# Thin products laid record by record among dense ones, in two stacked blocks of a fused three-layer model

## The reference

```python
# first block, twice: an RG-LRU branch and a sparse attention branch
h = rms_norm(x, norm_g); z = h @ w_in
y_a = rg_lru(causal_depthwise_conv(rg_x, conv_w, conv_b), ...) * silu(rg_gate)
y_b = nsa(q, k_c, v_c, k_s, v_s, k_w, v_w, br_gate, ...) * silu(nsa_gate)
x = x + concatenate([y_a, y_b]) @ w_out
# inside nsa: keys and values of 32 tokens at a time, every 16 tokens,
# go through w1 (2048 x 128) and w2 to 15 compressed keys and values for each of 2 groups
# second mixer: 8 heads of RWKV-7, 8 heads of attention with forget gates
q, k, v, f = split_cols(p_fox, FOX_SPLITS)          # f has 8 columns: the forget logits
bonus = jnp.sum(r_h * k_h * r_k, axis=-1, keepdims=True) * v_h
y = (y + bonus.reshape(B_, T_, RW_DIM)) * g
# then hierarchical_moe: 64 experts of 1024 x 512, top 2
```

## Time and profile before

| | |
|---|---|
| median of three runs | 1480.6 us (1480.16 to 1481.89) |
| the profiled execution's own time | 1476.84 us |
| its span, first to last instruction | 1475.1 us |
| PE busy | 1110.9 us, 75% |
| weight loads busy | 803.1 us, 54% |
| DVE, ACT, POOL busy | 344.5, 215.9, 68.4 us |
| mean granted TensorE clock | 0.901 |
| transferred | 463.41 MB at 314 GB/s |
| chain that ended last | DMA 54% of the span, PE 8% |

### The profile page before, as it was taken

The page is one execution under the profiler, slowest core; times in us unless marked ns, Lnnn a source line. Parts: engine busy times, 40 slices in busy tenths (PEclk is TensorE's granted clock), DMA queues, the critical chain, the costliest instruction groups (busy, mean ns, idle before and its releaser), DMA issues.

```text
span 1475.1 us, 35657 instructions
## 1 busy us (share of the span) xinstructions
PE 1110.9 (75%) x15914; PEld 803.1 (54%) x15914; DVE 344.5 (23%) x997; ACT 215.9 (15%) x594; POOL 68.4 (5%) x119
## 2 busy tenths in 40 slices
PE   7999999999998989866665666556665666556555
PEld 4886588654886757744444444444444444444443
DVE  2553236420574353111110111011101110111111
ACT  1162106310152111100000000000000000000000
POOL 1100010000110110000000000000000000000000
PEclk9999999999999889998888888888888888888898
DMA  8742234215110099999999999999999999999997
GB/s 285 267 137 91 88 114 172 87 65 180 58 58 4 4 393 394 427 428 428 428 428 429 428 428 429 430 427 428 430 429 427 427 431 428 428 427 431 427 427 320
DMA packets 69029, 463.41 MB, mean 314 GB/s; under 512 B 14789, under 2 KB 18278, under 8 KB 44390
## 3 DMA queue, kind: packets, MB, share of 16 engines
q1 hardware_dynamic: 64784, 459.76, 75.7%
q10 hardware_dynamic: 4182, 2.72, 0.7%
HBM read 461.41 MB, written 1.05 MB: 314 GB/s over the span
## 4 chain that ended last, share of the span: by engine, by line
DMA 54%; PE 8%; issue 0%; DVE 0%; ACT 0%; SPq 0%; POOLq 0%; DVEq 0%; POOL 0%
DMA weight_slots<-in_exp_w_down_dram 54%; PE bank L2347 4%; PE bank L2338 1%; PE bank L2330 1%; PE bank L2312 0%; PE bank L2298 0%; PE bank L2364 0%; ACT work_region L2268 0%; SPq L2182 0%; DVE normed_features L2469 0%; PE bank L2318 0%; DVE tokens L2547 0%; POOLq L2222 0%; DVE tokens L2529 0%; DVE tokens L2532 0%
## 5 line engine op out<-in xcount | busy, mean ns | idle before, releaser
L2338 PE MATMUL bank<-weight_slots,work_region 128*32 128x128 f32 x5120 | 184.2, 304 | 125.1 <-DMA weight_slots<-in_exp_w_up_dram 100.7
L2338 PEld LDWEIGHTS bank<-weight_slots,work_region 128*32 128x32 f32 x5120 | 158.3, 122 | 152.4 <-DMA weight_slots<-in_exp_w_up_dram 111.0
L2347 PE MATMUL bank<-weight_slots,work_region 128*32 128x256 f32 x1376 | 111.2, 477 | 90.4 <-DMA weight_slots<-in_exp_w_down_dram 89.0
L2338 PE MATMUL bank<-work_region 128*32 128x128 f32 x2560 | 92.7, 306 | 61.7 <-DMA work_region<-in_exp_w_up_dram 52.3
L2347 PEld LDWEIGHTS bank<-weight_slots,work_region 128*32 128x32 f32 x1376 | 57.2, 131 | 129.9 <-issue 90.5
L2338 PEld LDWEIGHTS bank<-work_region 128*32 128x32 f32 x2560 | 79.7, 123 | 75.4 <-DMA work_region<-in_exp_w_up_dram 57.4
L2268 ACT COPY work_region<-bank 128x256 f32<-128x256 f32 x64 | 23.8, 372 | 603.3 <-PE bank L2347 603.3
L2504 DVE TENSOR_SCALAR work_region<-work_region 128x128 f32<-128x128 f32 x128 | 38.5, 343 | 281.4 <-PE bank L2355 281.4
L534 PE MATMUL bank<-weight_slots,normed_features 128*128 128x512 f32 (+2 forms) x288 | 101.4, 509 | 2.3 <-DVE normed_features L792 2.3
L2347 PE MATMUL bank<-work_region 128*32 128x256 f32 x672 | 58.1, 499 | 45.2 <-DMA work_region<-in_exp_w_down_dram 44.5
L2515 DVE TENSOR_TENSOR work_region<-work_region,bank 128x128 f32<-128x128 f32 x64 | 23.9, 373 | 284.7 <-PE bank L2338 284.7
(11 more groups left out here) (429 smaller groups left out, 1218.4 us busy)
## 6 DMA issues: line engine op xcount, KB each, us to landing
weight_slots<-in_exp_w_up_dram SPq DMA_DIRECT2D x43, 2048.0 KB, 41.0
weight_slots<-in_exp_w_down_dram SPq DMA_DIRECT2D x43, 2048.0 KB, 40.7
weight_slots<-in_exp_w_gate_dram SPq DMA_DIRECT2D x43, 2048.0 KB, 41.7
work_region<-in_exp_w_gate_dram SPq DMA_DIRECT2D x21, 2048.0 KB, 41.8
work_region<-in_exp_w_up_dram SPq DMA_DIRECT2D x21, 2048.0 KB, 41.0
work_region<-in_exp_w_down_dram SPq DMA_DIRECT2D x21, 2048.0 KB, 40.6
weight_slots<-in_w_in_dram SPq DMA_DIRECT2D x16, 2048.0 KB, 10.0
weight_slots<-in_w_out_dram SPq DMA_DIRECT2D x6, 2048.0 KB, 8.4
```

The lines of the kernel that those rows point to most:

```text
L2338: mm = nc.tensor.matmul(B[bank][BLK * j:BLK * (j + 1), 0:P], x[:, c], w[u][:, c, j * P:(j + 1) * P], start=c == 0, stop=c == KC - 1, tile_ ...
L2347: mm = nc.tensor.matmul(B[7][BLK * j:BLK * (j + 1), 0:256], hidt[u][:, BLK * k:BLK * (k + 1)], w_down[u][:, k, j * 256:(j + 1) * 256], sta ...
```

## The change

Matmuls of few columns are issued between the matmuls of a dense product. The products are the same; their order on PE, and three waits, change.

- The last two of the four RG-LRU projections are written out chunk by chunk, and each chunk is followed by two matmuls of a compression: `compress(0)` goes with i = 2, `compress(1)` with i = 3. The waits for z, for ACT's copies out of B[0] and B[1], and for w1 move ahead of them. Nothing stands any more between the transposes and `score(0)`, nor between `lru_gates(0)` and `lru_gates(1)`.
- `rg_gate` is cut into single `features` products: the first goes behind `score(0)`, the second stays behind `turn_p(0)`, the third and fourth are mixed with the compressed scores of group 0 and 1, one chunk and one thin matmul in turn. `weigh(2)` and `weigh(3)` go behind them.
- In the second mixer each chunk of the value projection is followed by a matmul of the forget logits, and the wait for the low-rank weights moves ahead of it.
- The last quarter of the attention's output product (FO3) is done as chunk 2, half of the bonus, chunk 3, the other half.

```diff
                 for i in range(CT):
-                    mm = features(B[2 + i // 2][:, i % 2 * T:(i % 2 + 1) * T], chunk(RGX_S, 512), slice(i * P, (i + 1) * P))
-                    if i % 2:
-                        mm.then_inc(S["rgx_done"], 1)
+                    v = i - 2
+                    if v == 0:
+                        pe.wait_ge(S["z_ready"], was("z_ready") + 1)
+                        pe.wait_ge(S["qk_copied"], was("qk_copied") + 12)
+                    if v >= 0:
+                        pe.wait_ge(mem["w1_loaded"][v], weights)
+                    for c in range(KC):
+                        mm = nc.tensor.matmul(B[2 + i // 2][:, i % 2 * T:(i % 2 + 1) * T], chunk(RGX_S, 512)[:, c, i * P:(i + 1) * P], ht[:, c, :],
+                                              start=c == 0, stop=c == KC - 1)
+                        if c == KC - 1 and i % 2:
+                            mm.then_inc(S["rgx_done"], 1)
+                        if v >= 0:
+                            some = compress(v, range(2 * c, 2 * c + 2))
+                    if v == 1:
+                        some.then_inc(S["comp1_done"], 1)
...
-                pe.wait_ge(S["z_ready"], was("z_ready") + 1)
-                compress(0)
                 pe.wait_ge(S["qkt_ready"], was("qkt_ready") + 2)
                 score(0)
+                pe.wait_ge(S["qkt_ready"], was("qkt_ready") + 4)
+                pe.wait_ge(loaded[RGG_S], weights)
+                rg_gate(0)
                 pe.wait_ge(mem["small_in"], weights * 9)
                 pe.wait_ge(S["cv_ready"], was("cv_ready") + CT)
                 lru_gates(0)
-                compress(1).then_inc(S["comp1_done"], 1)
...
                 turn_p(0)
-                pe.wait_ge(loaded[RGG_S], weights)
-                rg_gate(0)
+                rg_gate(1)
                 turn_p(1)
...
-                rg_gate(1)
-                weigh(2)
-                weigh(3)
                 pe.wait_ge(S["kct_ready"], was("kct_ready") + 1)
                 for g in range(NG):
                     r = slice(64 * g, 64 * g + 64)
                     if g:
                         pe.wait_ge(S["cmp_scores"], was("cmp_scores") + 1)
-                    for m in range(MT):
-                        for j in range(HPG):
-                            at = g * P + (m * HPG + j) * 16
-                            mm = nc.tensor.matmul(B[1][:, at:at + NB], qt[r, m, j], kct[r, 0:NB], start=True, stop=True)
+                    for c in range(KC):
+                        i, (m, j) = 2 + g, divmod(c, HPG)
+                        gate = nc.tensor.matmul(B[0][:, i % 2 * T:(i % 2 + 1) * T], chunk(RGG_S, 512)[:, c, i * P:(i + 1) * P], ht[:, c, :],
+                                                start=c == 0, stop=c == KC - 1)
+                        at = g * P + (m * HPG + j) * 16
+                        mm = nc.tensor.matmul(B[1][:, at:at + NB], qt[r, m, j], kct[r, 0:NB], start=True, stop=True)
+                    if g:
+                        gate.then_inc(S["rgg_done"], 1)
                     mm.then_inc(S["cmp_scores"], 1)
+                weigh(2)
+                weigh(3)
...
             for m in range(MT):
-                mm = tokens(m, B[2][:, m * NH:(m + 1) * NH], w, slice(2 * LORA + P, LORA_W))
+                for c in range(KC):
+                    of = ht[:, c, m * P:(m + 1) * P]
+                    mm = nc.tensor.matmul(B[m][:, :], of, chunk(FV_S)[:, c], start=c == 0, stop=c == KC - 1)
+                    if c == KC - 1:
+                        mm.then_inc(S["fv_done"], 1)
+                    mm = nc.tensor.matmul(B[2][:, m * NH:(m + 1) * NH], of, w[:, c, 2 * LORA + P:], start=c == 0, stop=c == KC - 1)
...
+            fox_half(3, (2,))
+            bonus_of(0, B[item % 8])
+            end(fox_half(3, (3,)))
+            end(bonus_of(1, B[item % 8]))
```

More of the change, by code:

```diff
@@ L579, in _, with compress @@
                 pe.wait_ge(loaded[RGX_S], first_of_two)
-                for i in range(CT):
-                    mm = features(B[2 + i // 2][:, i % 2 * T:(i % 2 + 1) * T], chunk(RGX_S, 512), slice(i * P, (i + 1) * P))
-                    if i % 2:
-                        mm.then_inc(S["rgx_done"], 1)
+                def compress(v, some):
+                    for i in some:
+                        at = 448 + v * NG * NB
+                        mm = nc.tensor.matmul(B[1][:, at:at + NG * NB], w1_c[:, v, i], z[:, v, i], start=i == 0, stop=i == LP - 1)
+                    return mm
+                for i in range(CT):
+                    v = i - 2
[13 more added lines that the diff above has]
+                        some.then_inc(S["comp1_done"], 1)
                 pe.wait_ge(S["qk_ready"], was("qk_ready") + 1)
@@ L591, in _ @@
                     t.then_inc(S["qk_transposed"], 1)
[L593 to L598, removed]
                 def lru_gates(g):
@@ L604, in lru_gates, with rg_gate @@
                             mm.then_inc(S["lru_gates_done"], 1)
[L606 to L609, removed]
+                def rg_gate(i):
+                    mm = features(B[0][:, i % 2 * T:(i % 2 + 1) * T], chunk(RGG_S, 512), slice(i * P, (i + 1) * P))
+                    if i % 2:
+                        mm.then_inc(S["rgg_done"], 1)
                 def nsa_gate(m):
@@ L672, in _ @@
                 lru_gates(0)
-                compress(1).then_inc(S["comp1_done"], 1)
                 pe.wait_ge(S["tr_ready"], was("tr_ready") + CT)
                 lru_gates(1)
-                pe.wait_ge(S["qkt_ready"], was("qkt_ready") + 4)
                 score(1)
@@ L1398, in _ @@
                 pe.wait_ge(loaded[s], 16 * (DEPTH * uses + 1))
-                for m in range(0 if s == FV_S else 1, MT):
-                    if bank + m == 7:
-                        pe.wait_ge(S["params_ready"], 1)
-                    tokens(m, B[bank + m][:, :], chunk(s), slice(0, 512)).then_inc(done, 1)
+                if s == FV_S:
+                    continue
+                if bank == 6:
+                    pe.wait_ge(S["params_ready"], 1)
+                tokens(1, B[bank + 1][:, :], chunk(s), slice(0, 512)).then_inc(done, 1)
             pe.wait_ge(loaded[LORA_S], 16 * (DEPTH * 2 + 3))
@@ L1663, in _, with bonus_of @@
                 of_blocks(f"F5{m}", G[:, m], Q[:, m])
-            fox_last(3)
-            pe.wait_ge(S["rk_ready"], CT)
-            out = bank("BONUS")
-            for m in range(MT):
+            def bonus_of(m, out):
                 for i in range(CT):
@@ L1670, in _ @@
                     mm = nc.tensor.matmul(out[:, at:at + 2], rk[:, i, m * P:(m + 1) * P], const("head_pick"), start=True, stop=True)
-            end(mm)
+                return mm
+            pe.wait_ge(S["rk_ready"], CT)
+            item = ORDER.index("BONUS")
+            pe.wait_ge(*taken(item - 8))
+            fox_half(3, (2,))
+            bonus_of(0, B[item % 8])
+            end(fox_half(3, (3,)))
+            end(bonus_of(1, B[item % 8]))
             for m in range(MT):
```

## The result

The changed kernel takes 1490.1 us (median of 8 runs, 1485.4 to 1497.9), the kernel before on the same chip 1480.8 (8 runs). The ratio is 1.0063, with a 95% interval of 1.0041 to 1.0085: 9.3 us slower. I had forecast 1472.7 and a range up to 1480. The profiled execution is of 1490.2 us, span 1488.4; that of before was one of its faster ones (span 1475.1), so between the two profiles there are 13.3 us and not 9.3.

What follows compares the result with a forecast made beforehand. PE's path ahead of SP's weight release was taken as the bound, with DMA fixed behind it. Gains 3.25 + 1.5 + 4.7 + 0.1 = 9.55 us, less one clock fall of 1.7, gave -7.9: 1472.7 us, range 1467 to 1480.

Steps and rivals of the forecast that it cites:

- (e): Second half of each layer, turn_p(2) to turn_p(7) with scores mixed into the gate: gains 3.25 us (layer 0), 1.5 (layer 1).
- (a): Interleaving on PE: each dense-to-thin change saves 0.083 us, about 80 changes, 6.6 us less PE work.
- rival 1: Several weight loads run ahead under dense records, so more thin loads vanish: about 1467 us; chance 0.06.
- (b): PE clock: mixtures are over half dense, so none of eight half-clock stretches is expected, 13.7 us.
- rival 2: Clock falls return at the new waits or stay in the mixtures: 1477 to 1482 us, no change; chance 0.14.
- (c): Layer 1, first half: ACT's chain sets the pace, 15.0 us from lru_gates(0) to turn_p(2); 0.3 us gained.
- (d): Layer 0, first half: same offsets as layer 1, turn_p(2) at 92.45 against 94.46, 2.0 us gained.
- Rival 4: Gain doesn't arrive: ACT's chains 3 us longer in each layer, or later waits eat as much; 1479 us; chance 0.08.
- (f): Second mixer: logits end 1.25 us earlier and the 96 records behind them run at full clock; gain 4.7 us.
- (g): BONUS among the last output product: one dense-to-thin change, 0.1 us gained; no clock fall stood there.
- rival 3: A change of kind costs 0.08 us instead of saving 0.083, 13 us over 80 changes: 1486 us; chance 0.06.

Runs made afterwards that it cites:

- the version over 128 rows: Changed kernel with the thin compressed-score products reading all 128 rows instead of 64, same order and waits: 1481.9 us, ratio 1.0009.
- version with all runs cut: Kernel before with logits mixed, first compression mixed into the projection's last eighth, second in three pieces, compressed scores in two runs: 1465.6 us; repeated, 1467.8.
- The version cut in pieces: Kernel before with logits mixed and both compressions cut (first in the projection's last eighth, second in three pieces), compressed scores uncut: 1465.4 us, ratio 0.9901.
- the logits alone: Kernel before with only the forget logits laid among the value projection: 1476.2 us, ratio 0.9963.
- BONUS alone: Kernel before with only the BONUS products laid around the last output product: 1484.1 us, ratio 1.0016.
- the scores mixed alone: Kernel before with only the compressed scores laid among the gate's products: 1486.6 us, ratio 1.0047.
- the scores' runs cut: Kernel before with logits mixed and compressed scores in two runs of 8 products, gate and weighing between: 1479.1 us, ratio 0.9984.

## Why the prediction was wrong

**The step that failed** is in (e): "16 x 0.572 + 0.2". The overlap at a change from dense to thin was read at a change between two products of 128 rows (L602 to L597) and carried over to thin products of 64 rows. There the load doesn't slip under the dense record at all: 0.95 us a chunk instead of 0.572. The height was in sight all along, since the thin score products read qt[r] and kct[r] with r a slice of 64 rows. Against 0.655 apart this costs 0.295 x 32 = 9.4 us, and the runs give 9.2 (2 x 4.62). Weighed beforehand it would have turned the sign, from -7.9 us: the mixture by itself is +9.4 us. The Trainium skill (TensorEngine Tiling (Array Packing), Key Properties) says that changing the tiling mode, not just the tile, drains TensorE. By that rule a mixture of 64 and 128 rows drains it twice in every chunk, and the trace agrees, with 0.295 us for there and back; that the time goes into a drain, and not into something else that comes with the change of height, no run here shows.

**Step (a), 0.083 us a change: wrong, and worth 6.6 us.** One thin load is hidden, and the second dense record behind the thin ones starts 0.08 late. I had read the beginning of a run and its end (3.48 us for 32 records), but not the first dense record behind it; a mixture is made of these ends. With this term set to nothing the forecast lengths of both halves hold: layer 1's RGX to turn_p(2) is 41.01 + 1.33 = 42.3 (42.17 measured); turn_p(2) to turn_p(7) is 29.3 + 1.33 = 30.6, and the version over 128 rows takes 30.69. Of these 30.69 us PE waits 1.8 ahead of turn_p(7); at full clock the same products, apart, took 29.06 (version with all runs cut, layer 0). The Trainium skill's rule on weight loads that run ahead (TensorE: Matmul & The Clock Gate, part 2, step 1), which was rival 1, isn't borne out in its wide reading: no load but one is hidden, and even that is repaid.

**(b) the clock.** The eight old half-clock stretches are gone; three came in their place ahead of WU (two at 95.6 us behind the idle time ahead of turn_p(2), one at 293.5 behind that ahead of turn_p(7)), 5.1 us where I counted 1.7. That is rival 2 in part, at the places it named. **(c), (d)** ACT's chain: 14.8 us from lru_gates(0) at 80.04 to turn_p(2) at 94.88, 15.0 forecast; from the transposes to turn_p(2) 21.3, 21.4 forecast. Rival 4 is out. But the chain being right, the order was wrong: both compressions ahead of the transposes put 3.5 us on the path, and PE waits behind them for the same chain. The version cut in pieces, where one of them fills that wait, is 3.87 us a layer faster. **(f)** -3.4 by the profiles instead of -4.7: the clock's part came, the 1.25 us of overlap did not. **(g) BONUS**: -0.1 forecast; the ledger has +1.76 from the 96 records to WU, and in the profile an idle 1.96 us stands there. But the versions that leave BONUS as it was take up to 94.05 us for this stretch, over the changed kernel's 91.71, and the edit alone measured a ratio of 1.0016 (0.9993 to 1.0040): that the edit cost anything is not shown.

**Sum.** -7.85 (forecast) + 9.2 (change of height) + 6.6 (overlap paid back) + 3.4 (clock) + 1.9 (96 records to WU) = +13.2. The ledger has +1.3 ahead of RGX and -0.9 behind WU besides, where the kernels are the same: 13.6, against 13.3 us between the profiles. That it comes out so close owes something to luck, since the stretches behind 1.9, 1.3 and -0.9 vary by more than that from profile to profile; the terms that the experiments carry are the height and the overlap. Of the rivals, 3 had the right side, for a reason that is half right: a change of kind costs nothing among products of one height and 0.295 us there and back between two heights, nearly four times the 0.08 that rival 3 assumed.

Some of it stays open. Why half-clock stretches come in the first halves of the old order is not settled by these runs: with the same code from RGX to turn_p(2), the profiled executions of before, of the logits alone and of BONUS alone take 43.1, 43.2 and 45.9 us in layer 0 and 41.3, 41.3 and 43.1 in layer 1, and those of the scores mixed alone and of the scores' runs cut 42.9 and 43.2, then 47.3 and 47.3, with the clock at half for 17 us in a row; so it varies from execution to execution. Cutting runs helped at the compressions and not at the scores, and why is open too.

## What to carry to other kernels

Before products are interleaved, compare their operands' partitions: those with 64 rows among those with 128 cost about 0.3 us for each change there and back, and grouping them is the remedy; among products of one height, interleaving costs and saves nothing (0.88, 0.655 and 1.08 us a chunk here, mixed or apart). A wait that a new order brings can cost twice: in this kernel the clock fell behind such waits in several profiles. Narrow work is best spent as filler where the engine waits for another's chain, so find the waits first and cut the narrow run to their size. A saving read at the edge of a run must be followed past the next record of the other kind before it is multiplied.

## What the hardware showed that I had not expected

**Idle PE at every 256th record.** Between 440 and 535 us every idle time of PE of the kind "issue" that is longer than 0.25 us, in all fourteen profiles of this study, falls on one of its records 4545, 4801, 6593, 7361, 8129, 8385 and 8641 or the one behind it (counted from 0 over weight loads, matmuls and what its sequencer records between): each is 193 past a multiple of 256, whatever line it belongs to. They last 0.3 to 2.2 us, the longest behind runs of products of 64 and 32 columns, where 256 records pass in 1.2 to 1.3 us.

Of the kernel before, PE in order of time; these two stand in the middle of a run of one line that needs nothing from any other engine:

```profile
451.66 0.84 PE L1579 MATMUL bank<-weight_slots 64*32 64x64 f32 x63 [1.59 <-issue]
...
455.33 0.26 PE L1587 MATMUL bank<-work_region 32*32 32x32 f32 x8 [1.19 <-issue]
```

The traces also hold the packets that bring instructions, on a queue of their own: in the kernel before 50 packets of 16384 bytes, 0.82 MB. One begins ahead of each of these idle times, in the kernel before at 449.48, 452.79, 491.84, 509.56 and 513.20 us, for idle times that end at 451.66, 455.33, 494.74, 512.08 and 515.54. Over all profiles these idle times, 86 of them, end 2.2 to 2.9 us behind the start of such a packet.

The Trainium skill (Advanced Engine Details and Errata, ISA Cache) states a cache line of 16 KB, which is 256 instructions. The spacing and the size of the packets agree. If PE waits wherever it gets through a line before the next has come, all of this fits; but no run here moved a fetch, so that a late line is the cause stays an argument. It would explain why splitting BONUS changed the idle time: the three dense records that lay over record 6593 in before were moved off it. In the version with the logits alone, where BONUS is whole, that record waits 0.8 us.
